# RWKV's first step, the SSD's squares and the last step's low parts in a hybrid diffusion step on one core

## The reference, cut to what matters

```python
h = rms_norm(x, g1) * (1 + sc1) + sh1
u = h @ w_in                                   # split into SSD | RWKV | mLSTM
y_ssd = group_norm((y_f + y_b + d * xs) * silu(z), norm_g, 2, center=False)
y_ml  = group_norm(h_f + h_b, norm_g, heads, center=True) * sigmoid(o)
# RWKV, per token:  S = S*w - (S kk)(kk*a)^T + v k^T ;  o = S r
y_rwkv = group_norm(o_f + o_b, norm_g, heads, center=True) * gate
x = x + g1 * (concat(y_ssd, y_rwkv, y_ml) @ w_out)
x = x + g2 * ((silu(h2 @ w1) * (h2 @ w3)) @ w2)
```

## Time and profile before

| what | value |
|---|---|
| median of 3 runs | 2279.09 us (2275.01 to 2291.54) |
| time of the profiled execution | 2298.88 us |
| its span | 2296.9 us |
| PE busy | 2138.2 us (93% of the span) |
| DVE / ACT / POOL busy | 852.2 / 773.7 / 747.0 us |
| mean granted TensorE clock | 0.953 of full speed |

### The profile page before, as it was taken

The page is one execution under the profiler, slowest core; times in us unless marked ns, Lnnn a source line. Parts: engine busy times, 40 slices in busy tenths (PEclk is TensorE's granted clock), DMA queues, the critical chain, the costliest instruction groups (busy, mean ns, idle before and its releaser), DMA issues.

```text
span 2296.9 us, 46079 instructions
## 1 busy us (share of the span) xinstructions
PE 2138.2 (93%) x20508; PEld 1989.9 (87%) x20516; DVE 852.2 (37%) x1435; ACT 773.7 (34%) x1375; POOL 747.0 (33%) x551
## 2 busy tenths in 40 slices
PE   7999989888889999999979989988888899999999
PEld 6999756787789999999979987567778899999998
DVE  5845275546451111011138453754654311100112
ACT  4535453333242222121154364533332422222212
POOL 5422172224123333333323222621332233333331
PEclk7999997999989999999989999989999899999999
DMA  7543200000012222234326431000001122222221
GB/s 250 176 151 114 57 8 19 3 26 23 20 55 74 74 74 77 80 117 143 93 83 192 130 114 30 1 20 2 26 23 51 51 74 74 76 80 73 72 73 70
DMA packets 255259, 169.32 MB, mean 74 GB/s; under 512 B 23872, under 2 KB 228222, under 8 KB 255062
## 3 DMA queue, kind: packets, MB, share of 16 engines
q1 hardware_dynamic: 254835, 166.32, 24.4%
q10 hardware_dynamic: 227, 0.07, 0.0%
HBM read 162.21 MB, written 4.15 MB: 72 GB/s over the span
## 4 chain that ended last, share of the span: by engine, by line
PE 84%; DVE 6%; ACT 5%; issue 2%; POOL 1%; DMA 1%; SPq 0%; another core or an unknown queue 0%; DVEq 0%; ACTq 0%; POOLq 0%
PE PS L1010 21%; PE PS L1012 20%; PE PS L1011 20%; PE PS L1418 5%; PE PS L968 2%; ACT arena L1920 1%; POOL ring_r L694 1%; PE PS L1440 1%; PE PS L1076 1%; PE PS L1488 1%; PE PS L1298 1%; ACT whi_r L1749 1%; DVE U L2459 1%; PE PS L1233 1%; PE PS L1521 1%
## 5 line engine op out<-in xcount | busy, mean ns | idle before, releaser
L1010 PE MATMUL PS<-rwp_r,whi_r 128*128 128x320 f32 x2880 | 909.8, 316 | 46.0 <-POOL ring_r L694 21.2
L1012 PE MATMUL PS<-rwp_r,ring_r 128*128 128x320 f32 x2880 | 900.3, 313 | 0.0
L694 POOL TENSOR_TENSOR ring_r<-ring,whi_r 128x1024 fp32r<-128x1024 f32 (+1 forms) x204 | 500.1, 2453 | 1105.9 <-ACT whi_r L1749 1105.9
L1011 PE MATMUL PS<-arena_r,whi_r 128*128 128x320 f32 x2240 | 698.9, 312 | 0.0
L1010 PEld LDWEIGHTS PS<-rwp_r,whi_r 128*128 128x128 f32 x2880 | 550.9, 191 | 62.8 <-issue 29.4
L1012 PEld LDWEIGHTS PS<-rwp_r,ring_r 128*128 128x128 f32 x2880 | 550.4, 191 | 0.0
L1011 PEld LDWEIGHTS PS<-arena_r,whi_r 128*128 128x128 f32 x2240 | 427.4, 191 | 0.0
L1749 ACT ACTIVATE whi_r<-ring 128x1024 fp32r<-128x1024 f32 (+1 forms) x204 | 211.2, 1038 | 534.3 <-PE PS L1012 534.2
L1011 PE MATMUL PS<-U_r,whi_r 128*128 128x320 f32 x960 | 300.5, 313 | 0.0
L2701 DVE TENSOR_TENSOR U<-arena,PS 128x640 f32<-128x640 f32 x44 | 36.2, 822 | 551.6 <-PE PS L1012 551.6
L1011 PEld LDWEIGHTS PS<-U_r,whi_r 128*128 128x128 f32 x960 | 183.7, 191 | 0.2
(11 more groups left out here) (401 smaller groups left out, 2682.2 us busy)
## 6 DMA issues: line engine op xcount, KB each, us to landing
ring<-in_ffn_w SPq DMA_DIRECT2D x120, 512.0 KB, 3.8
rwp<-in_ada_w SPq DMA_DIRECT2D x64, 512.0 KB, 4.9
ring<-in_w_in SPq DMA_DIRECT2D x50, 512.0 KB, 5.0
U<-in_ada_w SPq DMA_DIRECT2D x16, 512.0 KB, 8.4
ring<-in_w_out SPq DMA_DIRECT2D x16, 512.0 KB, 4.1
arena<-in_ada_w SPq DMA_DIRECT2D x16, 512.0 KB, 4.8
ring<-in_ffn_w SPq DMA_DIRECT2D x16, 384.0 KB, 3.4
out<-arena SPq DMA_DIRECT2D x5, 512.0 KB, 2.6
```

What stands on the lines that cost most here:

```text
L694: g.tensor_tensor(rings_r[:, slot_of[n], 0:size(n), :], slot(n)[:, 0:size(n), :], whis[:, q % 2, 0:size(n), :].bitcast(F32), ALU.subtract) ...
L1010: mm(out, w[0][:, k, :], hi[:, cols], start=start, stop=False)
L1011: mm(out, w[0][:, k, :], lo[:, cols], start=False, stop=False)
L1012: return mm(out, w[1][:, k, :], hi[:, cols], start=False, stop=stop)
```

## The change

It has three parts.

1. POOL's `chunk_keys(0)` waits for `num_mm` instead of `yt_read`. PE turns the first keys before `mlstm_back(4)`, which moves behind them. Of the two `warm(8, 7)` the first goes, and the second becomes `warm(4, 2)`.
2. POOL adds the squares in pairs, one addition of 128x256 for each chunk behind `chunk_keys(0)`, and raises the new semaphore `ysq_sum`. PE waits for it and does 10 sums instead of 20.
3. In step 4 the low parts 0 to 3 stand together between `adds(3, 5)` and `adds(4, 7)`, and 4 and 5 stand behind the loop.

```diff
 def chunk_keys(k):
     if k == 0:
-        pool.wait_ge(s["yt_read"], at["yt_read"] + NC)
+        pool.wait_ge(s["num_mm"], at["num_mm"] + NC)
         pool.wait_ge(s["rw_ready"], at["rw_ready"] + 1)
...
 def rwkv():
     chunk_keys(0)
+    for c in range(NC):
+        pool.wait_ge(s["ysq_ready"], at["ysq_ready"] + c + 1)
+        g.tensor_tensor(U[:, Z:Z + 4:2, ck(c)], U[:, Z:Z + 4:2, ck(c)], U[:, Z + 1:Z + 4:2, ck(c)],
+                        ALU.add).then_inc(s["ysq_sum"], 1)
     for k in range(NC):
         chunk_levels(k)
...
     warm(6, 2)
-    mlstm_back(NC - 1)
...
-    pe.wait_ge(s["yt_read"], at["yt_read"] + NC)
+    pe.wait_ge(s["ys_read"], at["ys_read"] + NC)
     for k in range(NC):
         for d in range(2):
-            if i == 0:
-                warm(8, 7)
             pe.wait_ge(s["rw_keys"], at["rw_keys"] + i + 1)
...
             if i == 0:
-                warm(8, 7)
+                mlstm_back(NC - 1)
+                warm(4, 2)
+                pe.wait_ge(s["yt_read"], at["yt_read"] + NC)
             pe.wait_ge(s["rw_feat"], at["rw_feat"] + i + 1)
...
         if k == 0:
             pe.wait_ge(s["rw_tok"], at["rw_tok"] + 2)
-            pe.wait_ge(s["ysq_ready"], at["ysq_ready"] + NC)
+            pe.wait_ge(s["ysq_sum"], at["ysq_sum"] + NC)
             for c in range(NC):
-                for q in range(4):
-                    n = NC * (q // 2) + c
-                    ins = mm(PS[:, 0, n:n + 1], U[:, Z + q, ck(c)], ones[:, 0:1], start=q % 2 == 0,
-                             stop=q % 2 == 1)
+                for q in range(2):
+                    n = NC * q + c
+                    ins = mm(PS[:, 0, n:n + 1], U[:, Z + 2 * q, ck(c)], ones[:, 0:1], start=True,
+                             stop=True)
...
     # VectorE, step 4
-            for n in range(2):
-                y_low(n)
...
-        if k == 4:
-            y_low(2)
         for l in range(2):
             adds(3 + l, 5 + 2 * l)
...
-            if k == 4:
-                y_low(3 + l)
+            if l == 0 and k == 4:
+                for n in range(4):
+                    y_low(n)
...
-    y_low(5)
+    for n in range(4, 6):
+        y_low(n)
```

More of the change, by code:

```diff
@@ L113 @@
     "y_done": 8, "y_half": 4, "y_hi": 8, "y_lo": 8, "y_mm": 5, "ym_ready": 5, "yn_in": 64, "yn_mm": 2,
-    "yn_read": 2, "yn_rec": 1, "yn_std": 1, "yr_mm": 10, "yr_read": 10, "ys_read": 5, "ysq_ready": 5, "yt_mm":
-    5, "yt_read": 5,
+    "yn_read": 2, "yn_rec": 1, "yn_std": 1, "yr_mm": 10, "yr_read": 10, "ys_read": 5, "ysq_ready": 5, "ysq_sum":
+    5, "yt_mm": 5, "yt_read": 5,
 }
@@ L123 @@
     "pair_mm", "pair_read", "tmp_act", "tmp_dve", "feat_ready", "k_scaled",
-    "ysq_ready", "yn_mm", "yn_std", "yn_rec", "yn_read", "yn_in",
+    "ysq_ready", "ysq_sum", "yn_mm", "yn_std", "yn_rec", "yn_read", "yn_in",
     "rows_act", "rows_dve", "kk_sq", "lora_x", "rw_ready",
```

## The result

The changed kernel took 2258.46 us (median of 13 runs, 2248.74 to 2269.03), the kernel before beside it 2279.94 us (13 runs, 2273.87 to 2291.54). The ratio is 0.9886, interval 0.9861 to 0.9911. That is 26 us by the ratio, where 11.2 were forecast. The two medians themselves lie 21.5 us apart, a ratio of 0.9906, which the interval holds too; either way it is about twice the forecast. The time lies in the range 2256 to 2283. "Within 1%" had a chance of 0.88; by the ratio the gain is 1.1%, and the interval doesn't exclude a gain of just under 1%.

A forecast was written before the change was run, and what follows sets the result against it. PE was 84% of the chain, but an engine relay bounded the RWKV start and DVE's low parts delayed step 4. Gains of 8.6 and 3.3 minus 0.7 gave 11.2 us less: 2279.09 to 2268, range 2256 to 2283.

The forecast's parts named there:

- 8.6 + 3.3 - 0.7: Sum of gains at the RWKV start and in step 4, minus the loss behind the loop: 11.2 us less.
- Part 1 and 2, the start: mLSTM's end to inversion: earlier POOL keys, paired squares and halved sums save 4.1 us in layer 0, 4.5 in layer 1.
- about 15: Sign to look for: us from the six fillers to the inversion in layer 1, against 12.9 in layer 0.
- the 2.0 that was taken off for ACT and the clock: Layer 1's start: deducted from a 6.5 us gain, 0.7 for ACT's exponentials and the rest for PE's lower clock.
- The moved wait: PE's wait for `yt_read` behind the keys makes `mlstm_back`'s copy some 3 us later, but costs nothing.
- Part 3, step 4: Without two low parts ahead, `adds(1, 2)` and PE's third round start earlier: 1.65 us a layer, 3.3 in all.
- Behind the loop: Two DVE low parts beside POOL's L694 delay POOL by 0 to 0.72; 0.35 a layer, 0.7 us lost.
- 1.3 us of loss in layer 1: Layer 1's start: amount taken off because PE is expected at 1.2 GHz for part of the stretch.
- rival B: Clock stays up after the halved sums at the start: 4.7 us more gain, 2263.5 us; chance 0.13.
- rival C: PE falls to the lower clock before the sums and stays there in step 0: up to 2300 us; chance 0.07.
- A: POOL bounds the start more through DVE collisions: gain 2 a layer, 6.6 us less, 2272.5; chance 0.25 together with D.
- D: At the start PE waits for DVE, not keys; only halved sums won, 7.4 us less, 2272; chance 0.25 with A.

The follow-up runs named there:

- its two rows: The changed kernel measured twice, the second time with no edit: 2258.46 us (ratio 0.9886) and 2258.78 us (ratio 0.9874); at clock 0.965, 2263.0 and 2261.9 us.
- the second profile: The kernel before measured once more with no edit, for another profile: 2279.78 us, ratio 1.0008.
- with fillers: Changed kernel plus unread small matmuls in PE's two pauses of steps 0 to 3 (8 and 4): 2253.23 us, ratio 0.9868.
- with additions first: Changed kernel with POOL's additions for chunks 0 to 2 moved ahead of its keys: 2262.5 us, ratio 0.9887.

## Why the prediction was wrong

The step that failed is the clock in the sum 8.6 + 3.3 - 0.7. Away from the start the forecast put it at nothing, without a reason, and it priced step 4's pause at its length alone. The runs showed a mean clock 0.0066 higher in the changed kernel, worth 11.7 us, as much as the whole forecast, and they tie it to the closing of that pause.

The gain divides in two. At equal clock the changed kernel is 2276.4 - 2262.6 = 13.8 us faster (2262.6 is the mean of its two rows, weighted). Its clock is 0.9672 for 0.9606, which is 0.0066 x 1774 = 11.7 us. Together 25.5, the difference of the means (2284.2 and 2258.7), which they must add up to by the way they are made. At equal clock the parts add up too: parts 1 and 2 give 10.8 and part 3 alone 2.9, 13.7 for the 13.8.

**Part 1 and 2, the start: right, a little small.** Forecast 8.6 us. The distances gave 4.0 and 5.9, so 9.9, and 10.3 by the means of ten layers each; at equal clock parts 1 and 2 gave 10.8, with 0.7 us of error. By the ratios the parts add up (0.9956 x 0.9988 = 0.9944, and 0.9943 together), while the distances of single profiles don't (part 2 alone has 17.77 in layer 0, longer than the 17.0 of the earlier trace rows and shorter than the 19.2 of the second profile), since each hangs on where the clock falls in it. The terms held in sum, and their pieces less. POOL's 13 instructions took 9.71 us (380.33 to 390.04) and not 10.5, because collisions cost 0.74 and not 1.5; but the first key came 0.86 late in layer 0 too, where the 0.7 for ACT was counted in layer 1 alone. The Trainium skill's page "SBUF — State Buffer", section "Who interferes with whom", taken strictly, made the collisions 2.1. Instructions of 0.9 and more are there (L842 0.91, L2440 0.97), so the trace agrees that they collide. But four of POOL's instructions took 0.91 to 0.95, about 0.2 longer each and not 0.42, and it was mostly DVE that lost (0.83 to 0.97 for 0.42). The sums took 2.36, as forecast. The masks began 9.22 behind the fillers, forecast 9.1. In layer 1 "about 15" was 13.43: of the 2.0 that was taken off for ACT and the clock only 0.5 came.

**The moved wait: right in what it cost.** The copy came 3.1 us later. In layer 0 PE's weight loads for the products of keys and features (L1394) waited 0.42 for it, but the four fillers still ran in that time, and the sums behind the products had to wait 2.01 for POOL anyway. So nothing was lost.

**Part 3, step 4: the mechanism right, the size wrong.** Here the clock was left out first. "That is 1.65 us a layer" priced the pause and left out what the clock did behind it. Step 4 is 3.08 and 2.58 us shorter. Of this 1.4 to 1.5 is the low stretch of 570.10 to 573.50, which the fillers took away by themselves, and 1.1 to 1.7 the pause. Where neither a low stretch nor another pause stands in it, step 4 lasts 24.6 with the pause and 22.72 without (4 of the 12 layers with part 3), so the pause itself is worth 1.9; what PE idles in the other layers, with no releaser shown, was not explained. The low stretch could have been read from the 1.12 and 1.06 of L1418 behind the pause.

**Behind the loop: wrong, small.** Forecast 0.7 lost. DVE alone was late, POOL's 5.23 is the 5.24 of the earlier trace rows, and nothing was lost.

**What was missing from the sum: 11.7 us of clock.** The forecast treated the clock as a matter of the start (its 1.3 us of loss in layer 1, rival B's 4.7 of gain, rival C's loss). There it changed little. What lifts it is that step 4's pause is closed. Shown: filling that pause alone takes parts 1 and 2 from 0.9607 to 0.9675, with the same time at equal clock (2265.6 and 2265.7), and the kernel before from 0.9606 to 0.9651. The second pair isn't clean: at equal clock its time fell as well, by 2.8 us (2276.4 to 2273.6), where only the clock should have changed, so the division by the slope may be off by some 3 us. Not shown: how two pauses do so much. Two low stretches of 3.4 us at half speed are 0.0015 of the span's clock, at most a third of what is seen. The profiles don't place the rest. Their low time in stretches that no edit touches varies by tens of us from one execution to the next: in the 150 us ahead of layer 1's six fillers it is 38 to 49 us in six of the fourteen profiles and 0 to 7 in the other eight, and both kinds are found with the pause open and with it closed. One profile of a version can't show a difference of means, and the cause of the rest stays open.

**The rivals.** A needed a distance of 15 in layer 0; it was 13.0. D would have left 2.4 a layer at the start, where 4.0 and 5.9 came. B pointed the right way, but at another place and for another reason. C did not come. Behind the start the clock was low for 3.4 us in layer 0, and step 0 lasted 36.86 us for 38.33; in layer 1 39.11 for 41.42.

**The chances.** "Faster by over 1%" had 0.08. The 11.2 us were 0.5%, and all cases but C were built from the same two stretches, so they could not reach 1%. Two of their numbers are slightly off: B's 4.7 more than 11.2 give 2263.2, not 2263.5, and the bounds of the terms give 2263 to 2273, not 2261 to 2273. Neither matters beside the missing term. The measured 2258 is faster than every case named, B's 2263 among them. It lies in the range only by the margin that was left for an uncertain median, and that is luck. A case "the clock of the whole execution moves with the change" was missing on the fast side.

Adding to the changed kernel brought nothing that shows: 0.9868 with fillers, 0.9887 with additions first, beside 0.9874 in their batch.

## What to carry to other kernels

A pause of PE among small products, 1.7 us here, can be worth more than itself: look at the duration of the same matmuls behind it, and if they are nearly doubled, add the low stretch to the price. Where one execution's clock differs by 0.01 from the next, compare versions by mean clock over many runs, and at equal clock, before a difference of two profiles is explained.

## What the runs showed of the hardware

- The granted clock falls to 0.50 inside a step in which PE is busy for 32 of 37 us, and each such fall, 3.4 us long, costs 1.4 to 1.5 us. Whether it falls in a given step differs between executions of the same program: 6 of the 6 steps 1 to 3 in one profile of the kernel before, 1 of 6 in the next.
- The pause of 1.7 us in step 4 was followed by such a fall in 8 of the 10 layers that were profiled with it, in none of the 6 in which twelve matmuls of 256 columns, which nobody reads, stood in it, and in none of the 12 in which part 3 had closed it. Two of these six and two of these twelve had another fall, 2.2 and 2.3 us behind the mask, ahead of that place.
- The forty one-column passes of the sums took 4.83 us in the kernel before at a mean clock of 0.93, and 6.56 with part 1 alone at 0.68: products of one column pay for a low clock as well.
- Beside three of GpSimd's additions of 128x256 (2.20 us) a copy of VectorE of 128x2 took 0.51 us for 0.17, and two of its scalings of 128x128 took 1.39 for 0.48.
- Beside GpSimd's pair on L694 VectorE's two low parts took 5.46 us, where two of four took 1.5 of 3.02 in step 4, and GpSimd's pair did not get longer (5.23).
